# One 128-key score tile per query block in sliding-window attention, on one Trainium2 core

## Chip, core and metric

The kernel runs on one core of a Trainium2 chip. The metric is device time in microseconds (us) of one execution, the median of the runs shown. Five engines each work through a queue of their own in program order and meet only at semaphores: TensorE (PE; its weight loads are listed as PEld), VectorE (DVE), ScalarE (ACT), GpSimd (POOL) and SyncE (SP), which here only issues DMAs.

## The reference, cut to what matters

One decoder layer on 1024 tokens of width 1024: an RMS norm, one combined projection, two token mixers (four gated recurrence heads "HGRN2" and eight attention heads), an output projection into the residual, and a SwiGLU feed-forward part. The attention half, which is what changes here, is a sliding window of 128 keys, evaluated over blocks of 128 queries that each look at their own and the previous key block, with a learned sink that enters only the denominator:

```python
WINDOW = 128; BLOCK = 128                       # 8 query heads, 2 key/value heads of width 64
kb, vb = band(k), band(v)                       # [previous block, own block]: 256 keys per query block
scores = jnp.einsum('bnqhgd,bnkhd->bnhgqk', qb, kb)
rel = qpos - kpos
mask = (rel >= 0) & (rel < WINDOW) & (kpos >= 0)
scores = jnp.where(mask[None, :, None, None], scores, NEG_INF)
m = jnp.maximum(jnp.max(scores, axis=-1, keepdims=True), s)
p = jnp.exp(scores - m)
denom = jnp.sum(p, axis=-1, keepdims=True) + jnp.exp(s - m)
out = jnp.einsum('bnhgqk,bnkhd->bnqhgd', p / denom, vb)
```

Query q of a block sees the own block's key c where c <= q, and the previous block's key c where c > q. So of the two keys with the same column c exactly one is visible to each query: of 256 score columns 128 count. The first query block has no previous one.

## The kernel before, in words

**Order of work.** One list, written by schedule() (line 56), is walked by all engines. It mixes "dense" pieces (P, g, part: six matmuls of 128x512 of the input projection; g counts half tiles of 512 tokens) with the steps of the other stages. The attention has 16 units (SC 0 to SC 15): query block n = i // 2, and half of the heads, i % 2, four heads to a unit. Lines 127 to 130 lay the units out as a pipeline: step i of it does PV(i-4), TR(i-3), SN(i-2), SC(i), SE(i-1), in that order on every engine, and there is one dense piece to nearly every step:

```python
steps.append([s for s in (("PV", i - LAG - 1), ("TR", i - LAG), ("SN", i - 2), ("SC", i), ("SE", i - 1))
              if 0 <= s[1] < units])
order += mix(take(14), steps[:units]) + mix(take(4), steps[units:units + LAG])
```

There are 14 dense pieces to the first 16 steps, so two places have less: the first two units stand together, and PV 4 follows SC 7 without a dense piece between. At the end come P 15,0, then PV 12 and TR 13, P 15,1, then PV 13 and TR 14, P 15,2, then PV 14 and TR 15, P 15,3, and then H1 0, where the first recurrence head begins. The list before SC 0 ends with the key and query norms (AS, AD, AM, AN, AH, AL), and between them a stretch of dense work.

**A unit.** PE writes four heads' scores, 128 queries by 256 keys each, into PSUM banks 3 and 4 (SC, lines 1400 to 1404: 12 matmuls with a 64-row contraction, in three terms of a high/low split); it may do so once VectorE has read the unit before (semaphore s_masked). VectorE adds a mask of 0 and -1e30 and moves the sum to the SBUF tile sc (line 1753, 128x1024), takes row maxima (line 1756), joins the sink (1760) and forms the sink's argument (1762). In the next step ScalarE runs four exponentials with row sums in place (SE, line 934, 128x256 each) and one over the sinks (938). In the step after that VectorE adds up and inverts the denominators (SN, 1767, 1769), and GpSimd multiplies the probabilities (line 699, 128x1024). A step later PE transposes them (TR, line 1416: four blocks of 128x128 for the previous keys into bank 5, then four for the own keys into bank 6); ScalarE copies bank 5 (line 945) and VectorE bank 6 (line 1776) into pT, side by side. Last, PE multiplies both with the values (PV, line 1429) into bank 7, and ScalarE copies that out every second unit (line 951). The units 0 and 1, of the first query block, have 128 keys only, four transposes, and no copy on ScalarE. sc has three buffers, pT one.

**Between the stages.** DVE also scales each half tile of the dense work out of PSUM (line 1715), and splits weights (ACT line 896, DVE line 1684). At H1 (line 954) ScalarE loads another table of functions and runs three sigmoids (lines 961 to 963), the first as soon as the last half tile P 15 has been scaled out.

## Time and profile before

| what | us |
|---|---|
| runs (3) | 1156.22, 1156.56, 1158.71; median 1156.56 |
| the profiled execution | 1158.04, of which the span of its instructions is 1156.3 |
| PE busy | 1104.0 (95% of the span) |
| VectorE, ScalarE, GpSimd busy | 700.7, 502.7, 446.6 |
| mean granted TensorE clock | 0.994 of full speed |

Times in the trace are counted from the first instruction of the profiled execution. A group of instructions is a line of the kernel, an engine, an operation and its tiles (out<-in). The timeline gives the start, the duration, and in brackets how long the engine had been idle before it and whose signal ended that; an instruction that depends on nothing may start a little before the one in front of it is reported as ended. The ends of matmuls are modelled, so their starts are the surer measure.

### The profile page before, as it was taken

The numbers are of one execution on the slowest core, as the hardware profiler recorded it, in microseconds if no ns is written. First come the engines' busy times: TensorE is split into PE (matmuls) and PEld (weight loads), VectorE is DVE, ScalarE is ACT, GpSimd is POOL, SyncE is SP. The second block draws the span as 40 slices with busy tenths as digits, with TensorE's granted clock in tenths as the row PEclk, the third lists the DMA queues.
The fourth block names the chain that finished last, engine by engine and source line by source line (L and its number), as shares of the span: only waits on it lengthen the run. The fifth ranks groups of instructions, "written<-read, shape, count | busy, mean of one in ns | idle before, by whom it ended". The sixth has DMA issues, their size and how long they took to land.

```text
span 1156.3 us, 16822 instructions
## 1 busy us (share of the span) xinstructions
PE 1104.0 (95%) x6628; PEld 893.9 (77%) x6628; DVE 700.7 (61%) x870; ACT 502.7 (43%) x773; POOL 446.6 (39%) x348
## 2 busy tenths in 40 slices
PE   7999999989899999889899999999999999999998
PEld 7998766768677778657688888888888877888776
DVE  7214598596969895569524333433333497777786
ACT  8314466545365432446333333333333364454532
POOL 0301133363442430300653545455444744343452
PEclk9999999999999999999999999999999999999999
DMA  7101100010105102410331323133313493535433
GB/s 273 37 1 55 37 19 20 19 38 20 39 19 183 33 2 96 152 49 19 137 123 51 137 103 134 41 133 114 124 55 137 164 370 121 179 121 175 126 96 151
DMA packets 37102, 112.78 MB, mean 98 GB/s; under 512 B 4896, under 2 KB 9760, under 8 KB 35616
## 3 DMA queue, kind: packets, MB, share of 16 engines
q1 hardware_dynamic: 37024, 111.71, 28.6%
q8 instruction: 53, 0.87, 0.3%
q14 instruction: 25, 0.20, 0.1%
HBM read 83.12 MB, written 28.57 MB: 97 GB/s over the span
## 4 chain that ended last, share of the span: by engine, by line
PE 73%; DVE 11%; issue 5%; ACT 5%; POOL 3%; DMA 2%; SPq 0%; DVEq 0%; ACTq 0%; POOLq 0%
PE ps L1253 23%; PE ps L1255 22%; PE ps L1254 22%; DVE A L1835 1%; POOL D L727 1%; PE ps L1459 1%; DMA ubraw<-hidden 1%; PE ps L1416 1%; DVE M L1825 1%; PE ps L1429 1%; PE ps L1268 1%; DVE B L1792 1%; POOL sc L699 1%; DVE olo L1650 1%; DVE wlo L1684 1%
## 5 line engine op out<-in xcount | busy, mean ns | idle before, releaser
L1617 DVE TENSOR_TENSOR glo<-graw,ghi 128x1024 fp32r<-128x1024 f32 x21 | 26.2, 1247 | 147.4 <-POOL s34raw L646 147.4
L1253 PE MATMUL ps<-uhi,whi 128*128 128x512 f32 x272 | 113.7, 418 | 0.0
L1255 PE MATMUL ps<-uhi,wlo 128*128 128x512 f32 x272 | 107.1, 394 | 0.0
L1254 PE MATMUL ps<-ulo,whi 128*128 128x512 f32 x272 | 107.1, 394 | 0.0
L727 POOL TENSOR_TENSOR D<-B 128x1024 f32<-128x1024 f32 x28 | 64.2, 2294 | 41.3 <-DVE M L1825 22.0
L1965 DVE TENSOR_TENSOR yacc<-ps,yacc 128x512 f32<-128x512 f32 x104 | 68.7, 681 | 9.1 <-PE ps L1255 9.0
L1253 PE MATMUL ps<-ubhi,arhi 128*128 128x512 f32 x176 | 68.9, 392 | 2.0 <-DVE yacc L1965 1.9
L742 POOL TENSOR_TENSOR hst<-sg,up 128x512 f32<-128x512 f32 x21 | 29.0, 1383 | 103.7 <-issue 60.9
L1254 PE MATMUL ps<-ublo,arhi 128*128 128x512 f32 x176 | 68.5, 389 | 0.0
L1255 PE MATMUL ps<-ubhi,arlo 128*128 128x512 f32 x176 | 68.5, 389 | 0.0
L1933 DVE TENSOR_TENSOR ublo<-ubraw,ubhi 128x1024 fp32r<-128x1024 f32 (+1 forms) x44 | 50.8, 1161 | 27.5 <-ACT ubhi L1125 27.3
L639 POOL TENSOR_TENSOR s12raw<-uraw 128x512 f32<-128x512 f32 x21 | 28.2, 1341 | 99.6 <-DVE rec L1876 56.0
L1253 PE MATMUL ps<-ohi,s34hi 128*128 128x512 f32 x168 | 65.5, 390 | 0.8 <-ACT ps L1091 0.8
L1253 PE MATMUL ps<-ohi,ghi 128*128 128x512 f32 x168 | 65.5, 390 | 0.7 <-ACT ps L1082 0.7
L1253 PE MATMUL ps<-ohi,s12hi 128*128 128x512 f32 x168 | 65.6, 390 | 0.5 <-DVE s12lo L1623 0.5
L1254 PE MATMUL ps<-olo,s12hi 128*128 128x512 f32 x168 | 65.4, 389 | 0.0
L1254 PE MATMUL ps<-olo,ghi 128*128 128x512 f32 x168 | 65.4, 389 | 0.0
L1255 PE MATMUL ps<-ohi,s34lo 128*128 128x512 f32 x168 | 65.4, 389 | 0.0
L1255 PE MATMUL ps<-ohi,glo 128*128 128x512 f32 x168 | 65.4, 389 | 0.0
L1254 PE MATMUL ps<-olo,s34hi 128*128 128x512 f32 x168 | 65.4, 389 | 0.0
L1255 PE MATMUL ps<-ohi,s12lo 128*128 128x512 f32 x168 | 65.4, 389 | 0.0
L1253 PEld LDWEIGHTS ps<-uhi,whi 128*128 128x128 f32 x272 | 51.5, 189 | 12.5 <-issue 0.9
(287 smaller groups left out, 3064.2 us busy)
## 6 DMA issues: line engine op xcount, KB each, us to landing
hidden<-hst SPq DMA_DIRECT2D x11, 1792.0 KB, 6.0
ubraw<-hidden SPq DMA_DIRECT2D x33, 512.0 KB, 5.5
graw<-wg SPq DMA_DIRECT2D x21, 512.0 KB, 4.5
uraw<-wu SPq DMA_DIRECT2D x21, 512.0 KB, 3.6
wraw<-wproj SPq DMA_DIRECT2D x17, 512.0 KB, 3.6
araw<-wd SPq DMA_DIRECT2D x22, 384.0 KB, 4.9
x<-xT SPq DMA_DIRECT2D x8, 512.0 KB, 7.3
h<-xT SPq DMA_DIRECT2D x8, 512.0 KB, 5.6
```

The source lines that it names most:

```text
L639: nc.gpsimd.tensor_tensor(sw[:, 0:HALF], uw[:, 0:HALF], uw[:, HALF:D], ALU.add).then_inc(s_sum, 1)
L699: nc.gpsimd.tensor_tensor(probs, probs, rden[:, 4 * r:4 * r + 4].unsqueeze(2) .broadcast_to([P, GRP, n_keys]), ALU.mult).then_inc(s_prob, 1)
L727: nc.gpsimd.tensor_tensor(DD[lv % 2][:, :].rearrange("p (b l) -> p b l", l=2 * L), b4, mid, ALU.subtract).then_inc(s_lvs, 1)
L742: nc.gpsimd.tensor_tensor(hst[:, 4 if g % 2 else 7, :], sg2[:, :], upg[:, :], ALU.mult)\
L1253: nc.tensor.matmul(out, whi_, xhi_, start=first, stop=False, skip_group_check=seeded)
L1254: nc.tensor.matmul(out, whi_, xlo_, start=False, stop=False, skip_group_check=seeded)
L1255: return nc.tensor.matmul(out, wlo_, xhi_, start=False, stop=last, skip_group_check=seeded)
L1268: mm = nc.tensor.matmul(ps[:, 4 + x, :], ones[:, :], nsq[x][m][:, :], start=m == 0, stop=m == 7)
L1416: mm = nc.tensor.transpose(ps[:, 6 if cur else 5, j * P:(j + 1) * P], sc[:, i % 3, j, b * P:(b + 1) * P], ident[:, :])
L1617: nc.vector.tensor_tensor((glo2 if g == 2 else glo[g % 2])[:, :], graw[g % 2][:, :], ghi[g % 2][:, :].bitcast(F32), ALU.subtract).then_inc ...
L1933: nc.vector.tensor_tensor(ublo[j % 3][i][:, :, :], ubraw[j % 3][i][:, :, :], ubhi[j % 3][i][:, :, :].bitcast(F32), ALU.subtract).then_inc( ...
L1965: nc.vector.tensor_tensor(yacc[q][:, t, :], ps[:, bank, :], yacc[q][:, t, :], ALU.add).then_inc(s_dadd, 1)
```

## The change

A unit keeps one tile of 128 columns for its two key blocks. sc shrinks to [P, 3, GRP, P]. For units from 2 on, ScalarE copies the previous block's scores from PSUM to the tile, and VectorE then writes the own block's scores over it where c <= q (copy_predicated, with an int8 mask bandq). For units 0 and 1 GpSimd fills two buffers with -1e30 first. Maxima, exponentials, denominators and GpSimd's multiplication run on 128 columns a head. PE transposes four blocks instead of eight, into bank 5 or 6 by the parity of the unit. ScalarE copies the whole transposed tile into the left half of pT; VectorE multiplies the same bank with a 0/1 mask (band) into the right half, and ScalarE's copy now waits for that (s_pte1), as both read one bank. PV uses the previous block's values with the left half, and with the right half the difference of own and previous values (vstep), which GpSimd forms once, at SC 0, after the key norms. The mask wmask is replaced by band and bandq in GpSimd's set-up.

```diff
@@ -270,7 +271,8 @@
         kqhi = at("kqhi", 147, [P, 5, T], F32R)
         kqn = [at(f"kqn{i}", kb, [P, T]) for i, kb in enumerate((199, 107, 111, 115, 119))]
         kqlo = [at(f"kqlo{i}", kb, [P, T], F32R) for i, kb in enumerate((199, 107, 111, 115, 119))]
-        sc = at("sc", 167, [P, 3, GRP, 2 * P])
+        sc = at("sc", 167, [P, 3, GRP, P])
+        vstep = at("vstep", 183, [P, NC, P])
         asq = at("asq", 167, [P, 2, T])
         asqhi, asqlo = at("asqhi", 175, [P, T], F32R), at("asqlo", 179, [P, T], F32R)
         pT = at("pT", 179, [P, 2, GRP * P])
@@ -663,11 +658,12 @@
             step0(nc.gpsimd.memset(blk[0:HD, 0:HD], 1.0))
             step0(nc.gpsimd.memset(blk[HD:P, HD:P], 1.0))
 
-            step0(nc.gpsimd.memset(wmask[:, :], 0.0))
-            step0(nc.gpsimd.affine_select(out=wmask[:, :], in_=wmask[:, :], compare_op=ALU.is_gt, fill=NEG,
-                                          base=0, pattern=[[1, 2 * P]], channel_multiplier=-1))
-            step0(nc.gpsimd.affine_select(out=wmask[:, :], in_=wmask[:, :], compare_op=ALU.is_ge, fill=NEG,
-                                          base=P, pattern=[[-1, 2 * P]], channel_multiplier=1))
+            step0(nc.gpsimd.memset(band[:, :], 1.0))
+            step0(nc.gpsimd.affine_select(out=band[:, :], in_=band[:, :], compare_op=ALU.is_ge, fill=0.0,
+                                          base=0, pattern=[[1, P]], channel_multiplier=-1))
+            step0(nc.gpsimd.memset(bandq[:, :], 1.0))
+            step0(nc.gpsimd.affine_select(out=bandq[:, :], in_=bandq[:, :], compare_op=ALU.is_ge, fill=0.0,
+                                          base=0, pattern=[[-1, P]], channel_multiplier=1))
             step0(nc.gpsimd.memset(lmask[:, :, :], 0.0))
             for lv in range(LEVELS):
                 L = 1 << lv
@@ -693,15 +689,23 @@
                     nc.gpsimd.tensor_tensor(asq[:, i % 2, :], kq[:, i, :], kq[:, i, :], ALU.mult).then_inc(s_asq, 1)
                 elif step[0] == "SN":
                     i = step[1]
-                    r, n_keys = i % 3, nk(i)
+                    r = i % 3
                     pool.wait_ge(s_rden, i + 1)
-                    probs = sc[:, r, :, 0:n_keys]
+                    probs = sc[:, r, :, :]
                     nc.gpsimd.tensor_tensor(probs, probs, rden[:, 4 * r:4 * r + 4].unsqueeze(2)
-                                            .broadcast_to([P, GRP, n_keys]), ALU.mult).then_inc(s_prob, 1)
+                                            .broadcast_to([P, GRP, P]), ALU.mult).then_inc(s_prob, 1)
+                elif step == ("SC", 0):
+                    pool.wait_ge(s_ass, 10)
+                    nc.gpsimd.memset(sc[:, 0:2, :, :], NEG).then_inc(s_neg, 1)
+                    pool.wait_ge(s_an, 5)
+                    pool.wait_ge(s_vev, 2 * NC)
+                    kv = v[:, :, NH * P:2 * VW]
+                    nc.gpsimd.tensor_tensor(vstep[:, 1:NC, :], kv[:, 1:NC, :], kv[:, 0:NC - 1, :], ALU.subtract)\
+                        .then_inc(s_vstep, 1)
                 elif step[0] == "H1":
                     hh = step[1]
                     if hh == 0:
-                        pool.wait_ge(s_tr, tr_count(2 * NC - 1))
+                        pool.wait_ge(s_tr, 2 * NC)
                         nc.gpsimd.memset(A[:, :], 0.0).then_inc(s_setup, 1)
                     pool.wait_ge(s_sig, 3 * hh + 3)
                     gv = rawg[hh % 2]
@@ -926,12 +930,19 @@
                     i = step[1]
                     act.wait_ge(s_an, i + 1)
                     nc.scalar.activation(kqhi[:, i, :], kqn[i][:, :], ACT.Copy).then_inc(s_kqhi, 1)
+                elif kind == "SC" and step[1] >= 2:
+                    i = step[1]
+                    act.wait_ge(s_scm, i + 1)
+                    if i >= 3:
+                        act.wait_ge(s_tr, i - 2)
+                    nc.scalar.activation(sc[:, i % 3, :, :], ps[:, 3:5, :].rearrange("p b (j n) -> p (b j) n", j=2)[:, :, 0:P],
+                                         ACT.Copy).then_inc(s_prev, 1)
                 elif kind == "SE":
                     i = step[1]
-                    r, n_keys = i % 3, nk(i)
+                    r = i % 3
                     act.wait_ge(s_anm, i + 1)
                     for j in range(GRP):
-                        nc.scalar.activation(sc[:, r, j, 0:n_keys], sc[:, r, j, 0:n_keys], ACT.Exp,
+                        nc.scalar.activation(sc[:, r, j, :], sc[:, r, j, :], ACT.Exp,
                                              bias=nmax[:, 4 * r + j:4 * r + j + 1],
                                              accum_out=rsum[:, 4 * r + j:4 * r + j + 1]).then_inc(s_exp, 1)
                     act.wait_ge(s_asn, i + 1)
@@ -940,9 +951,9 @@
                 elif kind == "TR":
                     i = step[1]
                     if i >= 2:
-                        act.wait_ge(s_tr, tr_count(i) - 1)
+                        act.wait_ge(s_pte1, i + 1)
                         act.wait_ge(s_pv, i)
-                        nc.scalar.activation(pT[:, 0, :], ps[:, 5, :], ACT.Copy).then_inc(s_pte0, 1)
+                        nc.scalar.activation(pT[:, 0, :], ps[:, 5 + i % 2, :], ACT.Copy).then_inc(s_pte0, 1)
                 elif kind == "PV":
                     i = step[1]
                     if i % 2 == 1:
@@ -1406,16 +1417,13 @@
                 elif kind == "TR":
                     i = step[1]
                     pe.wait_ge(s_prob, i + 1)
-                    for b in range(nk(i) // P):
-                        cur = b == nk(i) // P - 1
-                        if cur and i:
-                            pe.wait_ge(s_pte1, i)
-                        if not cur and i > 2:
-                            pe.wait_ge(s_pte0, i - 2)
-                        for j in range(GRP):
-                            mm = nc.tensor.transpose(ps[:, 6 if cur else 5, j * P:(j + 1) * P],
-                                                     sc[:, i % 3, j, b * P:(b + 1) * P], ident[:, :])
-                        mm.then_inc(s_tr, 1)
+                    if i >= 2:
+                        pe.wait_ge(s_pte1, i - 1)
+                    if i >= 4:
+                        pe.wait_ge(s_pte0, i - 3)
+                    for j in range(GRP):
+                        mm = nc.tensor.transpose(ps[:, 5 + i % 2, j * P:(j + 1) * P], sc[:, i % 3, j, :], ident[:, :])
+                    mm.then_inc(s_tr, 1)
                 elif kind == "PV":
                     i = step[1]
                     n, pair = i // 2, i % 2
@@ -1424,10 +1432,13 @@
                     if n:
                         pe.wait_ge(s_pte0, i - 1)
                     pe.wait_ge(s_pte1, i + 1)
+                    if i == 2:
+                        pe.wait_ge(s_vstep, 1)
                     for t in range(0 if n else 1, 2):
                         for g in range(KVH):
-                            mm = nc.tensor.matmul(ps[HD * g:HD * g + HD, 7, pair * 2 * P:(pair + 1) * 2 * P],
-                                                  v[:, n - 1 + t, NH * P + HD * g:NH * P + HD * g + HD],
+                            vals = (vstep[:, n, HD * g:HD * g + HD] if n and t else
+                                    v[:, max(n - 1, 0), NH * P + HD * g:NH * P + HD * g + HD])
+                            mm = nc.tensor.matmul(ps[HD * g:HD * g + HD, 7, pair * 2 * P:(pair + 1) * 2 * P], vals,
                                                   pT[:, t, g * 2 * P:(g + 1) * 2 * P],
                                                   start=(t == 0 or n == 0), stop=(t == 1))
                     mm.then_inc(s_pv, 1)
@@ -1741,16 +1752,18 @@
                                             ALU.subtract).then_inc(s_kqlo, 1)
                 elif kind == "SC":
                     i = step[1]
-                    r, pair, n_keys = i % 3, i % 2, nk(i)
+                    r, pair = i % 3, i % 2
                     dve.wait_ge(s_scm, i + 1)
+                    sv = sc[:, r, :, :]
+                    pv = ps[:, 3:5, :].rearrange("p b (j n) -> p (b j) n", j=2)
                     if i == 0:
                         dve.wait_ge(s_setup, 1)
-                    if i >= 3:
-                        dve.wait_ge(s_tr, tr_count(i - 3))
-                    sv = sc[:, r, :, 0:n_keys]
-                    pv = ps[:, 3:5, :].rearrange("p b (j n) -> p (b j) n", j=2)[:, :, 0:n_keys]
-                    mv = wmask[:, 2 * P - n_keys:2 * P].unsqueeze(1).broadcast_to([P, GRP, n_keys])
-                    nc.vector.tensor_tensor(sv, pv, mv, ALU.add).then_inc(s_masked, 1)
+                        dve.wait_ge(s_neg, 1)
+                    if i >= 2:
+                        dve.wait_ge(s_prev, i - 1)
+                    cur = pv[:, :, P:2 * P] if i >= 2 else pv[:, :, 0:P]
+                    nc.vector.copy_predicated(sv, bandq[:, :].unsqueeze(1).broadcast_to([P, GRP, P]), cur)\
+                        .then_inc(s_masked, 1)
                     dve.wait_ge(s_masked, i + 1)
                     nm = nmax[:, 4 * r:4 * r + 4]
                     nc.vector.tensor_reduce(nm, sv, AX.X, ALU.max, negate=True).then_inc(s_amx, 1)
@@ -1770,10 +1783,12 @@
                     dve.wait_ge(s_rden, i + 1)
                 elif kind == "TR":
                     i = step[1]
-                    dve.wait_ge(s_tr, tr_count(i))
+                    dve.wait_ge(s_tr, i + 1)
                     if i:
                         dve.wait_ge(s_pv, i)
-                    nc.vector.tensor_copy(pT[:, 1, :], ps[:, 6, :]).then_inc(s_pte1, 1)
+                    nc.vector.tensor_tensor(pT[:, 1, :].rearrange("p (j q) -> p j q", q=P),
+                                            ps[:, 5 + i % 2, :].rearrange("p (j q) -> p j q", q=P),
+                                            band[:, :].unsqueeze(1).broadcast_to([P, GRP, P]), ALU.mult).then_inc(s_pte1, 1)
                 elif kind == "HK":
                     hh = step[1]
                     dve.wait_ge(s_sig, 3 * hh + 1)
```

## Rows read from the trace of the kernel before

**Rows 1.** Windows view: length, busy of PE, PEld, DVE, ACT, POOL (count); clock; DMA share; GB/s

```profile
141.00:216.00 75.00, 70.53 (x525) 49.37 (x526) 61.28 (x118) 47.51 (x168) 29.35 (x17) 1.00 0.05 15
```

**Rows 2.** Timeline of PE, one step in the middle: PV, TR, SC, dense, PV

```profile
173.02 1.08 PE L1429 MATMUL ps<-pT,v 128*64 128x256 f32 x8
174.04 1.10 PE L1416 MATMUL ps<-ident,sc 128*128 128x128 f32 x8
175.06 0.39 PE L1400 MATMUL ps<-kqhi 64*128 64x256 f32 x2
...
175.97 0.50 PE L1253 MATMUL ps<-uhi,whi 128*128 128x512 f32 x1
...
177.56 1.08 PE L1429 MATMUL ps<-pT,v 128*64 128x256 f32 x8
```

**Rows 3.** PE's waits, 140 to 222: two groups (idle before, releaser), two timeline pieces

```profile
L1416 PE MATMUL ps<-ident,sc 128*128 128x128 f32 x120 | 16.6, 280 | 3.7 <-POOL sc L699 3.6
...
L1400 PE MATMUL ps<-kqhi 64*128 64x256 f32 x64 | 10.7, 330 | 0.8 <-DVE sc L1753 0.8
...
169.50 1.09 PE L1416 MATMUL ps<-ident,sc 128*128 128x128 f32 x8 [1.08 <-POOL sc L699]
...
214.10 1.09 PE L1416 MATMUL ps<-ident,sc 128*128 128x128 f32 x8 [0.69 <-POOL sc L699]
```

**Rows 4.** Timeline of PE: unit 0, which has four transposes, then scores

```profile
147.50 0.64 PE L1416 MATMUL ps<-ident,sc 128*128 128x128 f32 x4
148.06 0.39 PE L1400 MATMUL ps<-kqhi 64*128 64x256 f32 x2
```

**Rows 5.** Timeline of DVE: unit 1 (128 keys) to the next work, then unit 9

```profile
143.61 0.69 DVE L1753 TENSOR_TENSOR sc<-ps,wmask 128x512 f32<-128x512 f32 x1
...
145.34 0.68 DVE L1715 TENSOR_TENSOR rawf<-ps,rs 128x512 f32<-128x512 f32 x1
...
176.18 1.23 DVE L1753 TENSOR_TENSOR sc<-ps,wmask 128x1024 f32<-128x1024 f32 x1
177.44 1.22 DVE L1756 TENSOR_REDUCE smax<-sc 128x4 f32<-128x1024 f32 x1
...
179.70 0.69 DVE L1776 COPY pT<-ps 128x512 f32<-128x512 f32 x1 [0.66 <-PE ps L1416]
```

**Rows 6.** Timeline of ACT: an exponential of unit 0, then a step in the middle

```profile
143.49 0.40 ACT L934 ACTIVATE sc<-sc,smax 128x128 f32<-128x128 f32 x1 [4.75 <-DVE smax L1760]
...
179.27 0.60 ACT L945 ACTIVATE pT<-ps 128x512 f32<-128x512 f32 x1 [1.88 <-PE ps L1416]
179.76 0.50 ACT L934 ACTIVATE sc<-sc,smax 128x256 f32<-128x256 f32 x1
```

**Rows 7.** Timeline of POOL: unit 0 (128 keys), unit 7 (256 keys)

```profile
146.38 1.04 POOL L699 TENSOR_TENSOR sc<-sc,smax 128x512 f32<-128x512 f32 x1 [14.82 <-DVE smax L1769]
...
176.22 1.90 POOL L699 TENSOR_TENSOR sc<-sc,smax 128x1024 f32<-128x1024 f32 x1 [2.65 <-DVE smax L1769]
```

**Rows 8.** View of line 1835: ns min/median/max, first and last start in us, form

```profile
L1835 DVE COPY_PREDICATED A<-lmask,ps x56: 710/726/736, 245.1 to 431.5; 128x512 f32<-128x512 int8 x56
```

**Rows 9.** Timeline of ACT at the seam to the recurrence

```profile
215.41 1.28 ACT L961 ACT_TABLE_LOAD   x1
217.34 1.06 ACT L961 ACTIVATE rawf<-rawf 128x1024 f32<-128x1024 f32 x1 [0.66 <-DVE rawg L1715]
```

**Rows 10.** Timeline of DVE and PE ahead of the first unit

```profile
136.36 1.28 DVE L1729 SCALAR_TENSOR_TENSOR kqn<-kq,small,ars 128x1024 f32<-128x1024 f32 x1 [2.40 <-ACT ars L924]
...
138.77 1.23 DVE L1740 TENSOR_TENSOR kqlo<-kqn,kqhi 128x1024 fp32r<-128x1024 f32 x1 [0.53 <-ACT kqhi L928]
...
140.83 0.38 PE L1400 MATMUL ps<-kqhi 64*128 64x256 f32 x2
```

**Rows 11.** Timeline of POOL and DVE in the recurrence: two SBUF inputs on both

```profile
242.16 1.90 POOL L727 TENSOR_TENSOR D<-B 128x1024 f32<-128x1024 f32 x1 [1.16 <-DVE rec L1816]
...
242.81 1.80 DVE L1825 TENSOR_TENSOR M<-K,D 128x512 f32<-128x512 f32 x1
```

More of the change, by code:

```diff
@@ L224, in build @@
         blkr = at("blkr", 1, [P, P], F32R)
-        wmask = at("wmask", 1.5, [P, 2 * P])
+        band = at("band", 1.5, [P, P])
+        bandq = at("bandq", 2, [P, P], I8)
         lmask = at("lmask", 2.5, [P, LEVELS, P], I8)
@@ L377, in build @@
         s_exp, s_den, s_rden, s_prob = sem("att_exp"), sem("att_den"), sem("att_rden"), sem("probs")
+        s_neg, s_prev, s_vstep = sem("scores_at_neg"), sem("prev_scores"), sem("value_steps")
         s_tr, s_pte0, s_pte1 = sem("probs_t"), sem("probs_t_prev_evac"), sem("probs_t_cur_evac")
@@ L420, in build @@
         N_CONST = 6
-        def nk(i):
-            return P if i < 2 else 2 * P
-        def tr_count(i):
-            return i + 1 if i < 2 else 2 * i
         def unit_used(u):
@@ L991, in _ @@
                     if lv == 0:
-                        act.wait_ge(*((s_lmm, 14 * hh) if hh else (s_tr, tr_count(2 * NC - 1))))
+                        act.wait_ge(*((s_lmm, 14 * hh) if hh else (s_tr, 2 * NC)))
                         nc.scalar.activation(M[1][:, :], DD[0][:, :], ACT.Exp, scale=-1.0).then_inc(s_lve, 1)
```

## The prediction

> **What bounds the kernel now.** I looked for the stage first, then for the engine that is late in it. The window that holds the attention is 75 us of the span, at a granted clock of 1.00: PE is busy 70.5 of it and VectorE 61.3 [rows 1], so both could set its pace, and the share alone does not say which. The timeline of PE does. In a step in the middle each piece follows the one before without a wait: PV, 1.02 later TR, 1.02 later SC, 0.91 later the dense piece, 1.59 later the next PV, 4.54 us in all [rows 2]. Meanwhile VectorE sits idle 0.66 and ScalarE 1.88 until PE's transposes land [rows 5, 6]. So from unit 9 to unit 15 PE's own work is the limit. Ahead of that and behind it others are late: in the whole stage PE stood 3.6 us before transposes that waited for GpSimd's multiplication, and 0.8 before the scores of unit 1 [rows 3]. One of these waits, 1.08, falls where no dense piece covers it, another, 0.69, before the last unit [rows 3]. At the end of the stage ScalarE's sigmoid waits for the last dense half tile [rows 9].
>
> A sum for the whole stage is then: what PE no longer does, plus the waits that go, less those that come.
>
> **PE.** Eight transposes take 1.02 to the scores behind them [rows 2], four take 0.56 [rows 4]: 0.46 less for each unit from 2 on. Between unit 0 and the start of TR 15 thirteen such units lie (2 to 14), so 13 x 0.46 = 6.0 us. PV keeps its eight matmuls (other values, same shapes), scores and dense pieces stay. The pace of a step falls to 4.54 - 0.46 = 4.08.
>
> **VectorE.** The masked addition of 1.23 becomes a copy_predicated of 128x512 from PSUM; the same form, int8 mask and PSUM data, takes 0.726 in the recurrence, and 0.736 at most [rows 8]. The maxima of 1.22 [rows 5] halve their columns. Unit 1 shows the narrow chain whole: from its addition of 0.69 to the next work 1.73 [rows 5]; with 0.726 for 0.69 that is 1.77. The multiplication by band has the form of that narrow addition (PSUM and a broadcast SBUF mask), 0.69, the same as the copy it replaces [rows 5]: nothing.
>
> **GpSimd.** The multiplication goes from 1.90 to 1.04 [rows 7]. This takes 0.86 from the path from denominators to transposes, on which the waits of rows 3 hang. I count all 3.6 of these as gone. GpSimd started 2.18 after TR (174.04 to 176.22) [rows 2, 7]; with 0.46 less of transposing that is 1.72, and with 1.04 and a signal the next transposes can start 2.8 after the last. PE needs 3.2 for what lies between them even where there are no scores (0.56 + 1.59 + 1.02). A signal between engines I put at 0.06, an allowance of mine; within VectorE the step from 176.18 + 1.23 to 177.44 shows 0.03 [rows 5].
>
> **ScalarE.** It gains a copy of 128x512 from PSUM, 14 times; the transposed tile's copy, same size, takes 0.60 and lets the next start after 0.49 [rows 6]. The copy reads strided from two banks, which no row shows on ScalarE; from below it costs 0.60, from above twice that if each bank were a copy of its own. I take 0.60, the row with the same bytes. The exponentials go from 0.50 to 0.40 [rows 6], so ScalarE's sum for a step hardly moves. Behind the new wait for scores stand the four exponentials of the unit before, and behind these VectorE's denominators; those are wanted only a step later.
>
> **The new loop.** ScalarE's copy of the transposed tile now waits for VectorE, the copy of scores stands behind it on ScalarE, and VectorE's overwrite waits for that: 0.69 + 0.06 for band and its signal, 0.49, 0.60 + 0.06 for the copy of scores, and 1.77, together 3.67 us from one step to the next. This is under PE's 4.08 by 0.4, so in the middle it hides. s_masked also comes later, some 2.4 after the scores start (0.91 for the scores, 0.66, 0.73 and signals), but PE asks for it a step later.
>
> Where the cover is thinner it shows. (a) SC 1 waits for the overwrite of unit 0: 0.8, as before. (b) PV 4 comes 0.56 + 0.91 = 1.47 after TR 4; four transposes land 0.66 after their start (PE's next TR starts 1.02 after 177.56, and VectorE's copy at 179.70, less 0.46) [rows 2, 5], so the pT that PV 4 needs is ready 0.66 + 0.75 + 0.66 = 2.07 after TR 4 if VectorE is free. Counted through step by step it is still at unit 6 for 0.5, since the list puts a half tile to scale out in front: I take 1.1, between 0.6 and 1.7. (c) PV 13 comes 0.56 + 1.59 = 2.15 after TR 13 against the same 2.07 plus what VectorE still has of unit 15: I take 0.5, between 0 and 1. Together 2.4.
>
> **GpSimd's preparation.** Filling two buffers and forming vstep falls into 14.82 us in which GpSimd is idle [rows 7]. vstep can start when VectorE's last norm ends, at 137.64 [rows 10]; 896 columns at the rate between the two rows of GpSimd are 1.68, so to 139.3. Over this VectorE starts kqlo at 138.77, two SBUF inputs, and PE's first scores at 140.83 wait for it [rows 10]. The recurrence shows what such a pair does: 1.80 for 512 columns while GpSimd reads [rows 11], which take 0.69 elsewhere [rows 5]. So kqlo may end at 139.3 + 1.23 = 140.6 instead of 140.0, still ahead of 140.83; if the strided vstep took half a microsecond more, 0.4 us would come through. I take nothing, and 0.5 at the other end. The Trainium skill says the same in SBUF — State Buffer, section Who interferes with whom: a VectorE instruction with two SBUF inputs and a GpSimd instruction that reads SBUF exclude each other for a whole instruction. It speaks against putting vstep there, and the trace agrees; by it the sum would be smaller by 0 to 0.5. The set-up masks at the start of the program are as many short instructions as those they replace, and nobody waits for them for tens of microseconds.
>
> **Sum.** At TR 15: 6.0 + 3.6 + 0.8 - 2.4 = 8.0. Behind it the sigmoid started 3.24 after TR 15 (217.34 - 214.10) [rows 3, 9]. Now the band product, ScalarE's copy and only then the table load come first: 0.66 + 0.75 + 0.60 + 1.28 and signals, 3.4, which takes back 0.15. What follows is the same list in the same dependence, so it moves as a block. The gain is 7.8 us: 1158.04 - 7.8 = 1150.2 for the profiled execution, which stood 1.48 above the median of the runs; on the median 1156.56 - 7.8 = 1148.8. With both waits of (b) and (c) at nothing it is 9.4, and 10 if the table load did not matter and the dense piece behind TR 15 counted; at their upper ends 6.7.
>
> **Rivals.** (1) *The loop becomes the bound.* If ScalarE's strided copy costs up to twice its 0.60, the loop is 3.67 + 0.5 = 4.2 and passes 4.08; worse, the waits (b) and (c) and the ones at the start grow with it. Each 0.1 us of loop above 4.08 costs about 1.3 over 13 units; a loop of 4.3 leaves 7.8 - 2.9 - 1 = 4 us: 1152.6. For it: two cross-engine signals more in the loop, and scaling and weight splits (0.6 to 1.2 each) that fall into it. Against it: 0.4 of slack, and rows of the same size for every link. (2) *The gain is taken back behind the stage.* The recurrence starts on a chain of ScalarE and VectorE; if something there, a weight load or a different phase of the clock, does not move along, less than 2.3 us is left: about 1156. Against it: every load in that stretch is released by a semaphore of the same list. (3) *Slower: VectorE and ScalarE take turns for longer than PE's old step.* Its place is the same loop; the price is about 13 us for each microsecond above 4.54, and it decides from a loop longer than the one here by 0.9: for instance a copy at 1.2 together with an overwrite at 1.2. At a loop of 5.0 the time is 1148.8 + 13 x 0.92 + 1 = 1161.8. Against it stands the row of copy_predicated, 56 times within 0.03 us [rows 8]. (4) *PE was not the limit in the middle.* The Trainium skill, in Trainium Kernel Development and Optimization, Performance Expectations, warns that matmul busy time misleads, and that weight-load busy is the better measure. Here that is 49.4 of 75 [rows 1]. That is a mechanism too: if PE had reserve in the middle, the six steps there would stay at 4.54, and 6 x 0.46 of the gain would be missing, which leaves 5.0: 1151.6. Against it: PE's starts follow each other without a wait, while both readers of its results stand idle [rows 2, 5, 6]. That the change does less than it says can be left aside: only units 0 and 1 go without the copy, and the shapes are in the diff.
>
> **How the numbers follow.** The forecast (gain 6 to 10) has 0.73, rival (1) 0.13, rival (2) 0.08, rival (3) 0.04, rival (4) 0.02. A measurement of this kernel can tell about 0.2%, 2.3 us, from no change. Faster by more: 0.73 + 0.13 + 0.02 = 0.88; within: 0.08; slower by more: 0.04. The range reaches from the gain of 10 (1146.5) over rival (4) to the better half of rival (1) (1153.0), which leaves out 0.06 + 0.08 + 0.04, about 2 in 10.
>
> **What would show it.** Right: steps of about 4.1 us between the scores of units 9 to 15, PE without waits there, transposes x64 instead of x120, copy_predicated at 0.73, ScalarE's score copy at 0.60, and TR 15 some 8 us earlier. Wrong: PE waiting at SC or PV in every step of the middle, for VectorE's overwrite or for ScalarE's pT copy, which is rivals (1) and (3); or TR 15 early and the sigmoid, or the first scan behind it, not, which is rival (2).

## The result, and the profile of the changed kernel

The changed kernel takes **1149.93 us** at the median of four runs (1149.61 to 1150.82); the kernel before, on the same chip, 1157.13 (1156.22 to 1158.71). The ratio is **0.9934, 95% interval 0.9918 to 0.9949**: 7.2 us faster, where 7.8 was forecast. The profiled execution took 1149.67 with a span of 1148.0.

The whole kernel hides the change: parts of it that the change does not touch differ by a microsecond from one execution to the next. So I measure one stretch, from PE's first scores (unit 0) to the start of ScalarE's first sigmoid (rawf). Before it runs from 140.83 to 217.34 [rows 9, 10], 76.51 us; after, from 141.00 to 210.11, **69.11**. This yardstick is used for every kernel below.

The windows view of the changed kernel, its attention stage (columns as in [rows 1]; the stretch is shorter, since the stage now ends near 208):

```profile
141.00:208.00 67.00, 64.32 (x468) 43.34 (x469) 46.62 (x118) 46.48 (x180) 17.23 (x17) 1.00 0.05 17
```

PE is busy 96% of it, against 94% in [rows 1], while VectorE falls from 82% to 70%. PE's own step is read from its timeline, with the same pieces as in [rows 2]:

```profile
175.28 0.66 PE L1425 MATMUL ps<-ident,sc 128*128 128x128 f32 x4
175.87 0.39 PE L1411 MATMUL ps<-kqhi 64*128 64x256 f32 x2
...
176.77 0.50 PE L1264 MATMUL ps<-uhi,whi 128*128 128x512 f32 x1
...
178.37 0.65 PE L1441 MATMUL ps<-pT,v 128*64 128x256 f32 x4
178.85 0.60 PE L1441 MATMUL ps<-pT,vstep 128*64 128x256 f32 x4
179.39 0.66 PE L1425 MATMUL ps<-ident,sc 128*128 128x128 f32 x4
```

From TR to TR 4.11 (175.28 to 179.39), where it was 4.54; no bracket stands behind a row, so nothing is waited for. From transposes to scores it is 0.59, and it was 1.02. Where PE does wait, the groups of PE's instructions between 140 and 222 us show, and the two timeline rows behind them:

```profile
L1411 PE MATMUL ps<-kqhi 64*128 64x256 f32 x64 | 10.6, 329 | 0.9 <-DVE sc L1765 0.8
L1425 PE MATMUL ps<-ident,sc 128*128 128x128 f32 x64 | 10.5, 287 | 0.0
L1441 PE MATMUL ps<-pT,v 128*64 128x256 f32 x64 | 10.4, 404 | 1.9 <-ACT pT L956 1.7
...
166.07 0.65 PE L1441 MATMUL ps<-pT,v 128*64 128x256 f32 x4 [1.18 <-ACT pT L956]
...
202.51 0.65 PE L1441 MATMUL ps<-pT,v 128*64 128x256 f32 x4 [0.55 <-ACT pT L956]
```

The 3.7 us ahead of transposes [rows 3] are gone, 0.0 in their place. New are 1.9 ahead of PV, 1.18 of it at PV 4 and 0.55 at PV 13, both for ScalarE's copy of pT. The groups of the other engines give the prices (busy us, mean ns):

```profile
L1765 DVE COPY_PREDICATED sc<-bandq,ps 128x512 f32<-128x512 int8 x16 | 11.8, 738 | 13.2 <-ACT sc L938 12.1 <-PE ps L1415 1.1
L1789 DVE TENSOR_TENSOR pT<-ps,band 128x512 f32<-128x512 f32 x16 | 11.0, 688 | 5.1 <-PE ps L1425 4.8
...
L956 ACT ACTIVATE pT<-ps 128x512 f32<-128x512 f32 x14 | 8.4, 598 | 15.6 <-DVE pT L1789 15.6
L938 ACT ACTIVATE sc<-ps 128x512 f32<-128x512 f32 x14 | 8.3, 592 | 2.3 <-PE ps L1415 2.3
...
L695 POOL TENSOR_TENSOR sc<-sc,smax 128x512 f32<-128x512 f32 x16 | 16.7, 1042 | 49.8 <-DVE smax L1782 49.8
```

The 12.1 us in the first row and the 15.6 in that of L956 are the new loop at work: VectorE waits for ScalarE's copy of scores in all 14 units, ScalarE for VectorE's band product in all 14. Two turns of the loop stand in VectorE's timeline, one in which VectorE has nothing else to do, and one in which it also scales a half tile (rawq):

```profile
166.59 0.73 DVE L1765 COPY_PREDICATED sc<-bandq,ps 128x512 f32<-128x512 int8 x1 [0.96 <-ACT sc L938]
...
168.36 0.69 DVE L1789 TENSOR_TENSOR pT<-ps,band 128x512 f32<-128x512 f32 x1
...
170.30 0.73 DVE L1765 COPY_PREDICATED sc<-bandq,ps 128x512 f32<-128x512 int8 x1 [0.97 <-ACT sc L938]
...
177.92 0.74 DVE L1765 COPY_PREDICATED sc<-bandq,ps 128x512 f32<-128x512 int8 x1 [0.97 <-ACT sc L938]
...
179.69 0.68 DVE L1726 TENSOR_TENSOR rawq<-ps,rs 128x512 f32<-128x512 f32 x1
...
182.22 0.74 DVE L1765 COPY_PREDICATED sc<-bandq,ps 128x512 f32<-128x512 int8 x1 [0.97 <-ACT sc L938]
```

3.71 us from overwrite to overwrite in the plain turn, 4.30 in the one with a half tile, and 4.84 where VectorE splits weights (190.24 to 195.08). In a plain turn PE's 4.11 is the longer of the two, and the idle time of VectorE and ScalarE costs nothing there. In sum the cover is thin: the ten turns from the overwrite of unit 5 to that of unit 15 take 40.79 (158.58 to 199.37), and the loop's own length in them, six plain turns, three with a half tile and one with weights, is 40.0. So the loop has 0.8 us to spare in ten turns, and not 0.4 in each. The seam, in ScalarE's timeline, and the preparation, in those of GpSimd and VectorE:

```profile
208.19 0.60 ACT L956 ACTIVATE pT<-ps 128x512 f32<-128x512 f32 x1 [2.59 <-DVE pT L1789]
208.81 1.28 ACT L972 ACT_TABLE_LOAD   x1
210.11 1.06 ACT L972 ACTIVATE rawf<-rawf 128x1024 f32<-128x1024 f32 x1
...
137.74 2.13 POOL L703 TENSOR_TENSOR vstep<-v 128x896 f32<-128x896 f32 x1 [2.63 <-DVE kqn L1740]
...
136.37 1.28 DVE L1740 SCALAR_TENSOR_TENSOR kqn<-kq,small,ars 128x1024 f32<-128x1024 f32 x1 [2.40 <-ACT ars L928]
...
138.79 2.16 DVE L1751 TENSOR_TENSOR kqlo<-kqn,kqhi 128x1024 fp32r<-128x1024 f32 x1 [0.53 <-ACT kqhi L932]
```

The sigmoid no longer waits for the dense half tile, as in [rows 9], but for pT and the table load behind it. And kqlo took 2.16, where it took 1.23 [rows 10].

### The profile page after: what moved, and what is told of

Same layout as the page of the kernel before. It is cut to its first block, busy times and chain, and to the rows that moved or that the text cites. A ratio compares the mean times of both kernels' runs of the same rounds, so it can differ in the third digit from the quotient of the medians.

```text
span 1148.0 us, 16740 instructions
## 1 busy us (share of the span) xinstructions
PE 1097.9 (96%) x6572; PEld 887.6 (77%) x6572; DVE 685.1 (60%) x870; ACT 502.8 (44%) x787; POOL 439.0 (38%) x351
## 4 chain that ended last, share of the span: by engine, by line
PE 73%; DVE 11%; ACT 5%; issue 5%; POOL 3%; DMA 1%; SPq 0%; DVEq 0%; ACTq 0%; POOLq 0%
PE ps L1264 23%; PE ps L1266 22%; PE ps L1265 22%; PE ps L1470 1%; POOL D L731 1%; DVE A L1850 1%; PE ps L1441 1%; DVE M L1840 1%; DVE B L1807 1%; DVE wlo L1695 1%; PE ps L1279 1%; DVE olo L1661 1%; DMA ubraw<-hidden 1%; PE ps L1425 1%; ACT ohi L888 1%
```

## The experiments

All of them start from the changed kernel. The stretch is that from the first scores to rawf, in the profile of each kernel; the last two columns are the median of its runs and the ratio to the kernel before on the same chip.

| kernel | stretch, us | to the changed kernel | median, us | ratio, 95% interval |
|---|---|---|---|---|
| before | 76.51 | +7.40 | 1157.13 | 1 |
| changed | 69.11 | 0 | 1149.93 | 0.9934 (0.9918 to 0.9949) |
| changed, once more | 69.09 | -0.02 | 1150.94 | 0.9931 (0.9917 to 0.9945) |
| eight transposes | 73.93 | +4.82 | 1157.52 | 0.9991 (0.998 to 1.0001) |
| score copy twice | 74.18 | +5.07 | 1156.32 | 0.998 (0.9965 to 0.9995) |
| score copy three times | 80.78 | +11.67 | 1163.25 | 1.0043 (1.0029 to 1.0058) |
| GpSimd's multiplication twice | 72.68 | +3.57 | 1153.19 | 0.9954 (0.994 to 0.9968) |
| denominators first | 73.00 | +3.89 | 1154.06 | 0.9961 (0.9948 to 0.9975) |
| denominators and left tile first | 67.60 | -1.51 | 1149.89 | 0.9927 (0.9915 to 0.994) |
| the same, value steps later | 67.58 | -1.53 | 1147.68 | 0.9908 (0.9894 to 0.9921) |
| the same, once more | 67.59 | -1.52 | 1149.39 | 0.9919 (0.9901 to 0.9937) |
| value steps later, alone | 69.07 | -0.04 | 1149.17 | 0.9916 (0.9893 to 0.994) |
| left tile first, old order | 68.32 | -0.79 | 1150.5 | 0.9924 (0.9902 to 0.9946) |

The repeats say what each column is good for: the stretch comes back within 0.02 us, the median within about 1 to 2.

**Is PE the limit in the middle?** PE transposes each tile twice, as many transposes as before; all else stays as in the changed kernel.

```diff
-                    for j in range(GRP):
+                    for j in range(GRP if i < 2 else 2 * GRP):
+                        j = j % GRP
                         mm = nc.tensor.transpose(ps[:, 5 + i % 2, j * P:(j + 1) * P], sc[:, i % 3, j, :], ident[:, :])
```

> The changed kernel with every unit from 2 on transposing its four blocks twice into the same place, so that PE again runs eight transposes a unit and nothing else changes. Theory A (PE sets the pace of the middle, and the eight transposes were its cost): the step of units 9 to 15 goes from 4.11 back to about 4.55; the waits at PV 4 and PV 13 shrink by about 0.5 each, since VectorE and ScalarE gain time; the end is 5 to 6 us later than in the changed kernel. Rival (VectorE and ScalarE set the pace already, PE had reserve): at most 1.5 us later.

PE's timeline of this kernel, one step:

```profile
172.61 0.38 PE L1411 MATMUL ps<-kqhi 64*128 64x256 f32 x2
...
176.13 1.10 PE L1426 MATMUL ps<-ident,sc 128*128 128x128 f32 x8
177.15 0.39 PE L1411 MATMUL ps<-kqhi 64*128 64x256 f32 x2
...
166.04 0.65 PE L1442 MATMUL ps<-pT,v 128*64 128x256 f32 x4 [0.55 <-ACT pT L956]
```

From scores to scores 4.54 (172.61 to 177.15), the old step to the hundredth, so PE had nothing in reserve. It also closes as a sum: 14 units by 0.43 are 6.0, from which the wait at PV 4 gives back 0.63 (1.18 to 0.55, as pT has longer) and that at PV 13, which is gone, 0.55: 4.8, and the stretch grew by 4.82. The ratios differ by more, 0.0057 or 6.6 us; what is beyond 4.8 lies outside the stretch, where executions differ.

**How long may the loop be?** ScalarE copies the scores once or twice more, into buffers that nobody reads.

```diff
+                    for c in range(1):
+                        nc.scalar.activation(spare[c][:, :, :], ps[:, 3:5, :].rearrange("p b (j n) -> p (b j) n", j=2)[:, :, 0:P],
+                                             ACT.Copy)
                     nc.scalar.activation(sc[:, i % 3, :, :], ps[:, 3:5, :].rearrange("p b (j n) -> p (b j) n", j=2)[:, :, 0:P],
                                          ACT.Copy).then_inc(s_prev, 1)
```

> The changed kernel with ScalarE copying the previous block's scores a first time into a spare tile, 0.49 us more in the loop of VectorE and ScalarE. Theory A: the loop grows from 3.70 to 4.19, just above PE's 4.11, so PE starts to wait at the scores by about 0.1 in plain steps and by 0.5 to 1.0 at the PV of steps in which VectorE also scales a half tile or splits weights; 4 to 6 us later than the changed kernel. Rival (the loop has cover to spare, the copies are hidden): under 1 us later.

> The same with two copies into spare tiles, 0.97 us more in the loop. Theory A: the loop is 4.68, above PE's old step of 4.54; PE waits 0.6 to 0.7 at nearly every step's scores; 10 to 12.5 us later than the changed kernel, that is 3 to 5 us slower than the kernel before. Rival (hidden copies): under 2 us later.

VectorE's timeline, two overwrites of the kernel with two copies, then PE's group for PV and its wait at PV 8:

```profile
172.38 0.73 DVE L1769 COPY_PREDICATED sc<-bandq,ps 128x512 f32<-128x512 int8 x1 [1.46 <-ACT sc L942]
176.57 0.74 DVE L1769 COPY_PREDICATED sc<-bandq,ps 128x512 f32<-128x512 int8 x1 [1.46 <-ACT sc L942]
...
L1445 PE MATMUL ps<-pT,v 128*64 128x256 f32 x64 | 10.4, 402 | 5.1 <-ACT pT L960 5.0
...
184.55 0.65 PE L1445 MATMUL ps<-pT,v 128*64 128x256 f32 x4 [0.43 <-ACT pT L960]
```

PE's groups and timeline, kernel with three copies:

```profile
L1415 PE MATMUL ps<-kqhi 64*128 64x256 f32 x64 | 10.7, 330 | 7.3 <-DVE sc L1769 7.2
...
L1445 PE MATMUL ps<-pT,v 128*64 128x256 f32 x60 | 9.8, 402 | 6.0 <-ACT pT L960 5.9
...
172.52 0.39 PE L1415 MATMUL ps<-kqhi 64*128 64x256 f32 x2 [0.61 <-DVE sc L1769]
...
177.20 0.39 PE L1415 MATMUL ps<-kqhi 64*128 64x256 f32 x2 [0.51 <-DVE sc L1769]
```

A plain turn of the loop is 3.71, then 4.19 (172.38 to 176.57), then 4.68 (172.52 to 177.20): some 0.49 for each copy, the distance at which the prediction put the next start behind it. With three copies PE waits for the overwrite in every step of the middle, and the kernel is slower than the one before: the prediction's third rival is a real mechanism, which this kernel misses by less than two copies. With two copies a plain turn passes PE's 4.11 by less than 0.1, yet the stretch grows by 5.07, three fifths of that at PV (the group there waits 5.1 in place of 1.9). The long turns are the reason. Besides PV 4 (1.43) and PV 13 (1.09), PE now waits at PV 2, 3, 8, 11 and 12, and each of these stands behind a band product that VectorE starts only after a weight split or a half tile (for PV 8 after the half tile at 182.54). The ten turns from the overwrite of unit 5 to that of unit 15 take 44.86 (159.21 to 204.07) instead of 40.79, which is 4.07 of the 5.07; ten times 0.48, less the 0.8 that these turns had to spare, gives 4.0. With three copies the same sum gives 8.9, and the ten turns grew by 8.88 (161.80 to 211.47). So the price begins before the plain turn is longer than PE's step; the kernel with denominators first, below, shows that with a plain turn of 4.08.

**What did the shorter multiplication on GpSimd bring?** GpSimd multiplies each unit twice, first into a spare buffer.

```diff
+                    nc.gpsimd.tensor_tensor(spare[:, :, :], probs, rden[:, 4 * r:4 * r + 4].unsqueeze(2)
+                                            .broadcast_to([P, GRP, P]), ALU.mult)
                     nc.gpsimd.tensor_tensor(probs, probs, rden[:, 4 * r:4 * r + 4].unsqueeze(2)
```

> The changed kernel with GpSimd multiplying each unit's probabilities a first time into a spare tile, so that its part takes 2.08 as it took 1.90 before. Theory A (GpSimd's shorter part is what removed PE's waits before transposes, at the start, at TR 5 and in the tail, and is worth nothing in the middle): PE waits again before TR 0, 3, 4, 5, 12, 14 and 15, by 0.2 to 0.9 each; 3 to 4 us later than the changed kernel; no waits at TR 6 to 11. Rival (GpSimd's time was hidden, only PE's work counted): under 0.5 us later.

PE's groups of this kernel:

```profile
L1428 PE MATMUL ps<-ident,sc 128*128 128x128 f32 x64 | 10.5, 287 | 4.1 <-POOL sc L698 3.6
L1444 PE MATMUL ps<-pT,v 128*64 128x256 f32 x64 | 10.4, 404 | 0.7 <-ACT pT L959 0.6
```

The waits ahead of transposes are back, 3.6 for GpSimd as in [rows 3], and those ahead of PV fall from 1.9 to 0.7, since transposes that come late give pT time. The stretch grew by 3.57. So waits of this size do hang on GpSimd's 0.86. That the two sums agree to a tenth is in part luck: the waits stand at TR 0, 3, 5, 12, 14 and 15, where the kernel before has them at TR 2, 3, 5, 14 and 15, and the stretch grew by 3.57 as 4.1 at the transposes, less 1.2 at PV, and some 0.7 that no listed wait holds.

**Are the new waits the loop's?** Two edits. The first puts VectorE's denominators and GpSimd's multiplication ahead of the transposes in the written order; the second cuts the loop: ScalarE copies the transposed tile first, and VectorE's band product waits for that.

```diff
-        steps.append([s for s in (("PV", i - LAG - 1), ("TR", i - LAG), ("SN", i - 2), ("SC", i), ("SE", i - 1))
+        steps.append([s for s in (("PV", i - LAG - 1), ("SN", i - 2), ("TR", i - LAG), ("SC", i), ("SE", i - 1))
...
-                        act.wait_ge(s_pte1, i + 1)
+                        act.wait_ge(s_tr, i + 1)
...
-                    dve.wait_ge(s_tr, i + 1)
+                    dve.wait_ge(*((s_pte0, i - 1) if i >= 2 else (s_tr, i + 1)))
```

The first edit alone:

> The written order puts the work for unit i-2's denominators (VectorE's sum and reciprocal, GpSimd's multiplication) ahead of the transposes of unit i-6 in every step; nothing else is changed. On VectorE the band product then stands behind the denominators, and these wait for ScalarE's exponentials. Theory A (PE's own work sets the pace where its operands come in time, 4.11 us a step; elsewhere the loop over VectorE's band product and ScalarE's two copies decides): the band product comes later by what the denominators take, so ScalarE's copy of the transposed tile is late for PV: waits of 0.3 to 1.2 at PV 3, 4, 8, 11, 12 and 13, in all 3 to 6 us slower than the changed kernel (1153 to 1156 against 1150). Rival B (GpSimd's multiplication, which now may start earlier, is what is late at the start of the stage): up to 1 us faster than the changed kernel, 1149.

VectorE's timeline, and PE's group for PV:

```profile
163.25 0.73 DVE L1765 COPY_PREDICATED sc<-bandq,ps 128x512 f32<-128x512 int8 x1 [1.22 <-ACT sc L938]
...
165.42 0.69 DVE L1789 TENSOR_TENSOR pT<-ps,band 128x512 f32<-128x512 f32 x1
...
167.33 0.73 DVE L1765 COPY_PREDICATED sc<-bandq,ps 128x512 f32<-128x512 int8 x1 [1.22 <-ACT sc L938]
...
L1441 PE MATMUL ps<-pT,v 128*64 128x256 f32 x64 | 10.4, 402 | 5.6 <-ACT pT L956 5.6
```

The band product starts 2.17 behind the overwrite instead of 1.77, a plain turn of the loop is 4.08, and PE waits 5.6 at PV instead of 1.9: 3.89 us lost, with nothing changed but the order. The ten turns take 43.75 (158.57 to 202.32), 2.96 more, where ten times 0.37 less 0.8 gives 2.9. Both edits:

> As the kernel with denominators first, and ScalarE copies the transposed tile as soon as PE has written it; VectorE's band product waits for that copy in place of the other way round. The loop from the overwrite over the band product and ScalarE's two copies back to the overwrite is then cut: ScalarE's copies hang on PE alone. Theory A (the waits at PV 4 and PV 13, 1.2 and 0.55 us, and the later table load come from that loop): no wait at PV 13, some 0.6 left at PV 4, ScalarE's table load 0.5 to 0.7 earlier behind TR 15, in all 1 to 2 us faster than the changed kernel (1148 to 1149 against 1150); in the middle the step stays 4.1. Rival C (ScalarE and VectorE are both late by their sums, whatever stands first): within 0.5 us of the changed kernel, the waits at PV only moved.

ScalarE's timeline, then PE's group for PV:

```profile
206.52 0.60 ACT L956 ACTIVATE pT<-ps 128x512 f32<-128x512 f32 x1 [2.63 <-PE ps L1425]
207.14 1.28 ACT L972 ACT_TABLE_LOAD   x1
208.63 1.06 ACT L972 ACTIVATE rawf<-rawf 128x1024 f32<-128x1024 f32 x1 [0.21 <-DVE rawg L1726]
...
L1441 PE MATMUL ps<-pT,v 128*64 128x256 f32 x64 | 10.4, 403 | 1.0 <-DVE pT L1789 1.0
```

ScalarE's copy now waits for PE and not for VectorE. The waits at PV fall by 0.9, and from TR 15 (205.83) to rawf it takes 2.80 instead of 3.39: 1.49 together, of a stretch shorter by 1.51. The second edit without the first:

> The changed kernel, with ScalarE's copy of the transposed tile ahead of VectorE's band product, and the written order as in the changed kernel (transposes ahead of denominators). Theory A: the band product now waits for ScalarE, and on VectorE the denominators stand behind it, so what the loop gave to PV is taken by GpSimd's multiplication: waits of about 0.4 at TR 5, 14 and 15 for GpSimd, the stretch from the first scores to ScalarE's rawf 68.9 (0.1 to 0.5 below the 69.1 of the changed kernel), and the 1.5 us of the kernel with both edits comes only when both are made. Rival E (the order is of no account, the swap alone brings it): 67.6, as with both.

PE's waits of this kernel (total, times, longest), in the stage:

```profile
PE ps L1441 <- DVE pT L1789: 0.8, 2, 0.6
PE ps L1425 <- POOL sc L695: 0.7, 3, 0.2
```

Half of the gain, 0.79. As expected PE now waits for GpSimd at three places, but 0.2 at each and not 0.4; I had also left out that the table load comes earlier here too. Each theory missed: the swap alone brings neither next to nothing nor all.

**Does preparing the value steps cost anything?** They wait for VectorE's kqlo instead of its last norm, first together with both edits above, then alone.

```diff
-                    pool.wait_ge(s_an, 5)
+                    pool.wait_ge(s_kqlo, 5)
```

> As the kernel with the left tile first, and GpSimd forms the value steps behind VectorE's last kqlo in place of beside it. If the two kept each other out for a whole instruction, kqlo takes 1.2 again in place of 2.16, the value steps 1.7 in place of 2.13, and the first scores start 0.1 to 0.2 earlier (140.8 to 140.9 in place of 141.0); if not, kqlo stays at about 2. In time no more than 0.2 us, below what the runs can tell.

> The changed kernel, with the value steps on GpSimd behind VectorE's last kqlo and nothing else. The kernel that had this together with the left tile first was 2.2 us faster at the median than the one without it. Theory A (GpSimd's value steps and VectorE's kqlo only keep each other out once): kqlo 1.2 instead of 2.16, the first scores 0.15 earlier than the changed kernel against the norms ahead of them, the stretch from the first scores to ScalarE's rawf the same 69.1 us; in time 0 to 0.3 us less than the changed kernel, 1150 to 1151, so the 2.2 was the difference between executions. Rival D (the place of the value steps is worth 2 us by itself): about 1148.

The second kernel's timelines, VectorE and GpSimd:

```profile
135.87 1.29 DVE L1740 SCALAR_TENSOR_TENSOR kqn<-kq,small,ars 128x1024 f32<-128x1024 f32 x1 [2.39 <-ACT ars L928]
...
138.28 1.23 DVE L1751 TENSOR_TENSOR kqlo<-kqn,kqhi 128x1024 fp32r<-128x1024 f32 x1 [0.53 <-ACT kqhi L932]
...
139.59 2.11 POOL L703 TENSOR_TENSOR vstep<-v 128x896 f32<-128x896 f32 x1 [4.98 <-DVE kqlo L1751]
```

kqlo is back at 1.23, so it had stood behind GpSimd's instruction: in the changed kernel it started 1.05 later than GpSimd (138.79 against 137.74) and ended 1.08 later (140.95 against 139.87), nearly its own 1.23. The value steps take 2.11 even with VectorE idle beside all but the last 0.4 of them; that they would take 1.7 was wrong. The stretch stays at 69.07; what is won lies ahead of it: from the last norm to the first scores 4.45 (135.87 to 140.32), against 4.63 in the changed kernel (136.37 to 141.00) and 4.47 before (136.36 to 140.83) [rows 10].

The first kernel's median was 2.2 us below that of the kernel without this edit, far more than the traces give it. So both it and the changed kernel were run again:

> The kernel with the left tile first and the value steps later, once more as it is. Theory A: 67.6 us from the first scores to ScalarE's rawf, and 1.5 to 2 us faster than the changed kernel (ratio to the kernel before 0.991 to 0.992); the further 1.5 us of the first measurement belonged to the stage behind it and don't come back. Rival D: ratio 0.9908 or less again.

> The changed kernel once more, as it is, beside the others on the same chip: 0.992 to 0.995 of the kernel before, waits of 1.1 to 1.2 at PV 4 and 0.5 to 0.6 at PV 13, steps of 4.11 in the middle.

It came to 0.9919 instead of 0.9908: a part of the 2.2 did not return, and its stretch is the same. In the stretch this version beats the changed kernel by 1.5 us in every profile. In the medians that is not shown: against the changed kernel they lean the same way (1.4 to 3 us on the ratios) with intervals that overlap, and against the kernel with the value steps alone, whose stretch is as long as that of the changed kernel, the repeat stands level on the same chip (1149.39 and 1149.17).

## Why the prediction was right

The mechanism and the size held. By its steps:

- **PE.** 0.46 a unit was forecast, and it was 0.43 (4.54 to 4.11): 13 x 0.43 = 5.6 instead of 6.0. The 0.56 from transposes to scores came from unit 0 [rows 4]; in the middle it is 0.59. Rival (4), PE with a reserve, fell with the doubled transposes. The Trainium skill (Trainium Kernel Development and Optimization, Performance Expectations) calls weight-load busy, and not matmul busy, a good measure of how close a kernel is to roofline. Read as a sign of reserve, as in this rival, it would have misled here: weight loads are busy 43.34 of 67, and still every row that PE lost in a plain step came out of the step.
- **Waits that go.** 3.6 and 0.8 were forecast. The first went in full, and the doubled multiplication brought as much back, though not all at the same places. The 0.8 at SC 1 was set against a wait (a) of the same size, and that came: 0.82.
- **New waits.** (b) PV 4 1.1 forecast, 1.18; (c) PV 13 0.5 forecast, 0.55. The group for PV holds 1.9.
- **The loop.** 3.67 forecast, 3.71 in a plain turn; ScalarE's strided copy from two banks 0.60 forecast, 0.592, copy_predicated 0.726 forecast, 0.738.
- **Value steps.** Nothing was forecast, between 0 and 0.5; 0.16 came through (4.63 against 4.47 from the last norm to the first scores), and with the value steps later it was gone. The rule that was weighed, from the Trainium skill's SBUF — State Buffer, Who interferes with whom, agrees with the trace: the later of the two instructions, kqlo, ended 1.08 after GpSimd's, nearly the 1.23 that it takes by itself.
- **Seam.** 3.4 forecast, 3.39 (206.72 to 210.11).

From the first scores to TR 15 it took 73.27 before (140.83 to 214.10) and 65.72 after: 7.55. The terms as measured give 5.6 + 3.7 + 0.8 - 0.8 - 1.9 = 7.4. Less the seam's 0.15 and the 0.17 ahead of the stage, rawf starts 7.23 earlier. The forecast was 7.8, and 0.4 of the 0.57 between them is PE's 0.46. The waits at PV (1.9 instead of 1.6) and the value steps (0.17 instead of nothing) add to it; 0.1 more of waits that went, and the 0.15 between 7.4 and 7.55, which stands in no term, take half of that back.

Where the prediction was loose is the slack of the loop. It set 3.67 against PE's 4.08 in every step, although rival (1) names the half tiles and weight splits that fall into the loop, and it priced only what passes 4.08, at 13 us for each microsecond, with the loss deciding from 4.54. At 4.19 the stretch grew by 5.07, where that price plus the 1 us for the other waits gives 2.4; at 4.68 by 11.67 instead of 8.8. Between these two it is 13.5 us for each microsecond, so the price held, and its start was wrong: the 0.4 is the slack of a plain turn, and the long turns use it up but for 0.8 us in ten. The change would stop paying well below 4.54: between 4.19 (2.33 of the 7.40 us left) and 4.68 (4.27 lost) a straight line, an estimate, gives 4.36. So "it hides" came true with a fifth of the margin that the prediction counted on, and that was in part luck.

Rival (2), a gain taken back behind the stage, did not happen: from rawf to the start of ScalarE's last squares for the norm behind the output projection (nsq, at 507.02 and 499.90 us), it took 289.68 before and 289.80 after. The 1.1 us more by which the profiled executions differ (8.37 in all, 7.23 at rawf) lie behind that, where the change has no part.

## What to carry to other kernels

When two engines form a loop beside the one that sets the pace, don't take the slack from a plain turn: add up the loop over all its turns, with the other work that its engines do in some of them. Here a plain turn had 0.4 us to spare and ten turns together 0.8, so nearly every tenth that a turn grew by came through. Of two readers of one tile, let the one go first behind which the loop's next link is queued; that swap, with a matching order, was worth 1.5 us of the stretch. And for changes below a per cent, measure the stretch between two rows that the change bounds: it came back within 0.02 us where the medians differed by 1 or 2.

## What the hardware showed besides

The same idle stretch of PE costs differently in different executions of one program. In the recurrence PE waits some 2.25 us for VectorE, in both executions of the changed kernel. The first, then the repeat: PE's timeline behind the wait, and the window (the granted clock is the third number from the end):

```profile
390.10 1.06 PE L1452 MATMUL ps<-ident,D 128*128 128x128 f32 x8 [2.25 <-DVE S L1859]
...
389.00:393.00 4.00, 2.90 (x17) 2.59 (x18) 4.00 (x6) 2.41 (x4) 1.76 (x1) 1.00 0.00 0
```

```profile
390.18 1.94 PE L1452 MATMUL ps<-ident,D 128*128 128x128 f32 x8 [2.24 <-DVE S L1859]
...
389.50:393.50 4.00, 3.32 (x13) 3.02 (x14) 4.00 (x6) 2.13 (x3) 1.30 (x1) 0.57 0.00 0
```

In the first execution the clock stayed at its upper level, 2.4 GHz (1.00); in the repeat it fell to 1.2 GHz behind the wait (0.57 over the window), and the same eight transposes took 1.94 instead of 1.06. Such falls come at different places from execution to execution: from 231.5 to 234 it is the first that was granted 0.50, and the repeat 1.00. Whether the 1 to 2 us by which medians differ are theirs was not shown. In the runs of the kernel before in the last series the two go together (a mean clock of 0.988 with 1163.47 us, 0.996 with 1156.77); in the four of the changed kernel they don't (0.991 with 1149.61, 0.996 with 1150.82).

GpSimd's value steps took 2.11 to 2.13 for 896 columns, read in rows of 128, where the 1024 columns of [rows 7, 11] take 1.90. It is 2.13 with VectorE's kqlo standing beside it and 2.11 with kqlo already done, so kqlo is not the reason; what is was not tried.
